# Combining the experts' rows: the second token tile's weighted sum formed on TensorE with diagonal matrices

## The chip, the core and the metric

The kernel runs as one program on one core of a Trainium2 chip. Its time is the device time of one execution in microseconds (us). A core has TensorE (PE in the rows: matrix products into PSUM; PEld is its weight load), VectorE (DVE), ScalarE (ACT), GpSimd (POOL) and SyncE (SP, which here issues the large transfers). Each runs its own instructions in order and waits on semaphores for the others.

## The reference, cut to what matters

Two layers of a diffusion trunk with 256 context and 256 latent tokens, width 1024, all float32. Each layer is an attention mixer and then a mixture of 16 experts, of which each token uses two. What the change touches is the last part of each layer:

```python
w = w / jnp.sum(w, axis=-1, keepdims=True)          # two weights for each token
y = jnp.zeros_like(h)
for e in range(N_EXPERTS):
    a = jax.nn.silu(h @ w_gate[e]) * (h @ w_up[e])
    y = y + gates[:, e:e + 1] * (a @ w_down[e])      # gates is zero but for the two chosen experts
...
x = x + g2 * y.reshape(b, n, d)
...
return rms_norm(x, final_norm_g)
```

So each token's new row is x + g2 * (w1 * y1 + w2 * y2), where y1 and y2 are the outputs of its two experts. Layer 0 does it for context and latent tokens, layer 1 for latent tokens only.

## The kernel before, in words

**Tiles and stages.** Tokens go in tiles of 128: four in layer 0 (two context, two latent), two in layer 1. A layer runs: modulated norm and its transposes (L1546), the QKV products (L1643, each float32 product as three of split parts), attention, the output projection (L1794), the router, the expert blocks (L1878), and then the combination.

**Expert blocks.** A loop over the experts takes blocks of 32 (token, choice) pairs. GpSimd gathers the rows of a block, TensorE multiplies, and GpSimd scatters the results (L766) to the DRAM tensor `expert_rows`. ScalarE copies the last block's result out of PSUM at L1060; TensorE's last work of the loop is two tiny products at L1951, and its last two waits there are for `m_ac` and `m_y`, the second of which is that copy.

**The combination.** When the last scatter has landed, SP issues four transfers of 512 KB (L690): y1 and y2 of tile 0, then y1 and y2 of tile 1, into `val[:, 0..3]`. For each of these two tiles ScalarE multiplies y1 by its per-token weight (`weigh_first`, L860), and VectorE then does three instructions over 128x1024 (`add_experts`): y2 * w2 + y1 (L1162), times the gate row (L1163), plus the kept residual (L1164). The residual of tiles 0 and 1 is kept meanwhile in PSUM banks 1, 2, 6 and 7; that of tiles 2 and 3 of layer 0 is kept in SBUF, in the tensor `moe`, and copied back by ScalarE at L1078. Tile 0 is finished before tile 1, on VectorE's own order. In layer 0 the rows of tiles 2 and 3 are loaded into the same places once tiles 0 and 1 are done (the semaphore `s_cb`), and those tiles are combined later, beside the next layer's products.

**What follows.** In layer 0 ScalarE and VectorE normalise the two context tiles (L837, L854, L1121, L1152, L1153), TensorE turns them (L1546) and starts the QKV products of layer 1. The weights of the first such group are split into two parts before the combination (ScalarE L470, VectorE L473). In layer 1 ScalarE squares the rows (L1092), takes a root (L1094), VectorE scales (L1540), and SP stores.

**Products that nobody reads.** `keep_busy(count)` (L1846) issues `count` products of 128x256 into PSUM bank 3. Their results are not read. The kernel before calls it three times in each layer, around the router.

One float32 product shows as two instructions in the trace: 64 output projection products of layer 0 stand as 128 records of L1794. TensorE's four products of the change, 128x512 each, are so eight records.

Of the kernel before, what the change touches and what calls it, by code (L numbers as in the profile page):

```python
# [31 lines left out]
ALU = mybir.AluOpType  # L32
ACT = mybir.ActivationFunctionType
X_AXIS = mybir.AxisListType.X

P = 128
# [4 lines left out]
LAYERS = 2  # L41
# [33 lines left out]
TILES_OF = [list(range(TILES)), list(range(CTX_TILES, TILES))]  # L75
# [53 lines left out]
def build_trunk(nc, x, c, ctx, c_ctx, ada_w, ada_b, norm1_g, norm2_g, final_norm_g, diff_w_qkv, diff_w_o,  # L129
# [3 lines left out]
    with ExitStack() as stack:  # L133
# [3 lines left out]
        def sem(name):  # L137
            return stack.enter_context(nc.semaphore(name))
# [21 lines left out]
        val = over("val", SET_KB[1] + 32, [P, TILES, D])  # L160
# [16 lines left out]
        resid = sb("resid", [P, TILES, D])  # L177
# [15 lines left out]
        wts = sb("wts", [P, 2, TILES])  # L193
# [4 lines left out]
        ps = stack.enter_context(nc.psum_tensor("ps", [P, 8, 512], F32))  # L198
# [23 lines left out]
        def row(l, piece, t):  # L222

            s = int(t >= CTX_TILES)
            return rows[:, 2 * (piece % 3) + s if l == 0 else LATENT_ROWS[piece]]
# [27 lines left out]
        blk_actT = moe_part(3328, FG).rearrange("p (k s) -> p k s", s=SLOTS)  # L253
        blk_out = [moe_part(3456 + b * DG, DG) for b in range(2)]

        def kept(l, m):

            if m < 2:
                return ps[:, (1, 6)[m]:(3, 8)[m]].rearrange("p a b -> p (a b)")
            return moe_part((m - 2) * D, D)  # L260
# [14 lines left out]
        ident = const("ident")  # L275
# [45 lines left out]
        s_oe = [sem(f"attended_copied_{l}") for l in range(LAYERS)]  # L321
        s_on = sem("heads_normalised")
        s_hs = sem("head_squares")
        s_w1 = [sem(f"first_experts_weighed_{l}") for l in range(LAYERS)]
        s_ot = [sem(f"o_turned_{l}") for l in range(LAYERS)]
        s_oc = [sem(f"o_turned_copied_{l}") for l in range(LAYERS)]
        s_rc = sem("sums_inverted")
        s_wm = [sem(f"wo_products_{l}") for l in range(LAYERS)]
        s_we = [sem(f"wo_added_{l}") for l in range(LAYERS)]
# [13 lines left out]

        s_extra = sem("extra_parts_loaded")
        s_keep = sem("residual_rows_kept")
        m_gu = [sem(f"block_gates_ups_{l}") for l in range(LAYERS)]
        m_dn = [sem(f"block_downs_{l}") for l in range(LAYERS)]
        m_xt = [sem(f"block_in_turned_{l}") for l in range(LAYERS)]
# [7 lines left out]
        s_yl = [[sem(f"expert_rows_loaded_{l}_{b}") for b in range(2)] for l in range(LAYERS)]  # L356
# [99 lines left out]
        def split_weights(eng, l, p, half):  # L456

            g = qkv_jobs[l][[pos[0] for pos in qkv_pos[l]].index(p)][0]
            st = at[l]["qkv", g]
            number = HALF_STRIPS * l + 2 * p + half  # L460
            high = w_high[(2 * p + half) % 3][:]
            ks = slice(half * KC // 2, (half + 1) * KC // 2)
            if eng is nc.scalar:
                wait_strip(eng, l, st)
                if half == 1 and p > 0:
                    eng.wait_ge(s_half, 6 * l + p)
                elif p > 1:
                    first = [pos[0] for pos in qkv_pos[l]].index(p - 1)
                    eng.wait_ge(s_qm[l], first)
                eng.copy(high, strip(l, st)[:, ks]).then_inc(s_whi, 1)  # L470
            else:
                eng.wait_ge(s_whi, number + 1)
                eng.tensor_tensor(w_low[:, strips[l][st][4], ks], strip(l, st)[:, ks], high,  # L473
                                  ALU.subtract).then_inc(s_wlo, 1)
# [73 lines left out]
        NT = [len(t) for t in TILES_OF]  # L548
        HALF = D // 2
# [284 lines left out]
        def _(act):  # L834
# [21 lines left out]
            def weigh_first(l, m):  # L856

                act.wait_ge(s_yl[l][m % 2], 32 * (m // 2 + 1))
                y1 = val[:, 2 * (m % 2)]
                act.activation(y1, y1, ACT.Copy, scale=wts[:, 0, m:m + 1]).then_inc(s_w1[l], 1)  # L860

            for a in range(ADA_QKV // 2):
                copy_mod(a)
# [6 lines left out]
            for l in range(LAYERS):  # L870
# [29 lines left out]
                for n, (g, t) in enumerate(qkv_jobs[l]):  # L900
# [7 lines left out]
                    if qkv_copy[l][n][0] == "act":  # L908
                        m = qk_index[l][n]
# [152 lines left out]
                gate = ps[:, 0, 0:FG]  # L1062
# [12 lines left out]


                for m in range(2, NT[l]):
                    act.copy(resid[:, TILES_OF[l][m]], kept(l, m))  # L1078
                if l == 0:
                    for half in range(2):  # L1080
                        split_weights(act, 1, 0, half)
                for m in range(2):
                    weigh_first(l, m)
                if l == 0:
                    for t in range(CTX_TILES):
                        act.wait_ge(s_cb[0], t + 1)
# [11 lines left out]
        def _(dve):  # L1098
            steps = [0]

            def step(ins):

                steps[0] += 1
                ins.then_inc(s_v, 1)
                dve.wait_ge(s_v, steps[0])
# [49 lines left out]
            def add_experts(l, m):  # L1155

                t = TILES_OF[l][m]
                if l == 0:
                    dve.wait_ge(s_rows, 16 * 8)
                dve.wait_ge(s_w1[l], m + 1)  # L1160
                y1, y2 = val[:, 2 * (m % 2)], val[:, 2 * (m % 2) + 1]
                step(stt(y1, y2, wts[:, 1, m:m + 1], y1, ALU.mult, ALU.add))  # L1162
                step(tt(y1, y1, row(l, 3, t), ALU.mult))  # L1163
                sync(tt(resid[:, t], kept(l, m) if m < 2 else resid[:, t], y1, ALU.add), s_cb[l])  # L1164

            def router_weights(l):
# [9 lines left out]
            for l in range(LAYERS):  # L1176
# [29 lines left out]
                for n, (g, t) in enumerate(qkv_jobs[l]):  # L1206
# [15 lines left out]
                    m = qk_index[l][n]  # L1222
# [301 lines left out]
                if l == 0:  # L1524
                    for half in range(2):
                        split_weights(dve, 1, 0, half)
                for m in range(2):
                    add_experts(l, m)
                if l == 0:
# [14 lines left out]
        def _(pe):  # L1544
# [43 lines left out]
            for l in range(LAYERS):  # L1588
# [363 lines left out]
                        .then_inc(count[l], 1)  # L1952
                pe.wait_ge(m_ac[l], 2 * pairs + 1)
                pe.wait_ge(m_y[l], 2 * pairs + 1)


_INS = ["x", "c", "ctx", "c_ctx", "ada_w", "ada_b", "norm1_g", "norm2_g", "final_norm_g", "diff_w_qkv", "diff_w_o",
# [18 lines left out]
```

## Time and profile before

| | us |
|---|---|
| median of three runs | 1184.06 |
| lowest, highest | 1183.81, 1190.32 |
| the profiled execution's own time | 1184.05 |
| its span in the trace | 1181.9 |

The 2.15 us between the profiled time and its span lie around the traced instructions. Busy time in the span: PE 982.5 us (83%), PEld 658.2, DVE 403.8 (34%), ACT 375.3 (32%), POOL 218.4 (18%). These shares are means over stages with different limits. The change is in two short stages, from about 667 to 688 us and from 1153 to 1178 us, in which TensorE has no work at all, so they are to be read by the chain of waits and in order of time.

### The profile page before, as it was taken

Reading aid. Unit: us, or ns where it says so; the run is one execution under the profiler, and the core shown is the slowest. Engines: PE = TensorE matmul, PEld = TensorE weight load, DVE = VectorE, ACT = ScalarE, POOL = GpSimd, SP = SyncE. Lnnn points to the kernel's source line nnn. Section 1 sums busy time; section 2 is a strip of 40 time slices with the busy share of each in tenths; the row PEclk is TensorE's granted clock in tenths of the full one; section 3 lists DMA queues with packets and bytes.
Section 4 is the critical chain, followed back from the end, with each engine's and each line's share of the span. In section 5 each row is a group of like instructions: output and inputs, shape, how many; then the busy total and the mean of one; then the engine's idle time right before and its main releaser. Section 6 shows DMA issues by size and latency. Waiting matters only on the chain.

```text
span 1181.9 us, 24437 instructions
## 1 busy us (share of the span) xinstructions
PE 982.5 (83%) x9596; PEld 658.2 (56%) x9597; DVE 403.8 (34%) x809; ACT 375.3 (32%) x803; POOL 218.4 (18%) x329
## 2 busy tenths in 40 slices
PE   3699999987789989899899569999999779876650
PEld 1477777544555666466576357787555646553320
DVE  1533330357733532122122373222854512121103
ACT  3532222466621222122222354234842112221102
POOL 0000000000000034244344201910000224442211
PEclk9899999999989999899899869999999889997875
DMA  9766665998230669999999467224447698999972
GB/s 339 254 221 228 226 218 177 335 368 322 88 136 21 220 236 368 422 421 422 425 422 395 171 223 169 72 72 159 198 127 319 262 413 341 411 423 426 424 316 112
DMA packets 93682, 322.07 MB, mean 272 GB/s; under 512 B 21241, under 2 KB 33954, under 8 KB 81330
## 3 DMA queue, kind: packets, MB, share of 16 engines
q1 hardware_dynamic: 85746, 305.40, 67.1%
q0 software_dynamic: 7008, 12.62, 2.9%
q10 hardware_dynamic: 864, 3.15, 0.7%
q8 instruction: 47, 0.77, 0.3%
q14 instruction: 17, 0.14, 0.0%
HBM read 313.67 MB, written 13.99 MB: 277 GB/s over the span
## 4 chain that ended last, share of the span: by engine, by line
PE 66%; DMA 16%; DVE 7%; issue 4%; ACT 3%; SPq 2%; POOL 1%; POOLq 0%; DVEq 0%; ACTq 0%
PE ps L1878 23%; PE ps L1643 21%; DMA expert_sets<-in_moe_w_up_dram 8%; PE ps L1794 7%; PE ps L1546 5%; PE ps L1570 3%; DMA expert_sets<-in_moe_w_down_dram 2%; DMA ring<-in_diff_w_qkv_dram 2%; PE ps L1696 2%; DMA ada_late<-in_ada_w_dram 2%; PE ps L1723 1%; PE ps L1752 1%; DMA expert_rows<-moe,scatter_idx 1%; SPq L590 1%; PE ps L1849 1%
## 5 line engine op out<-in xcount | busy, mean ns | idle before, releaser
L1878 PE MATMUL ps<-expert_sets,moe 128*32 128x256 f32 x6304 | 369.8, 396 | 77.3 <-DMA expert_sets<-in_moe_w_up_dram 47.1
L1878 PEld LDWEIGHTS ps<-expert_sets,moe 128*32 128x32 f32 x6304 | 241.2, 114 | 205.3 <-issue 100.4
L1504 DVE STREAM_TRANSPOSE moe<-moe 128x256 f32<-128x256 f32 x70 | 45.8, 655 | 324.8 <-PE ps L1878 303.1
L1643 PE MATMUL ps<-w_high,x_high 128*128 128x512 f32 x352 | 142.2, 404 | 7.6 <-DVE hT L506 2.7
L1643 PE MATMUL ps<-w_low,x_high 128*128 128x512 f32 x352 | 138.9, 395 | 0.0
L1643 PE MATMUL ps<-w_high,x_low 128*128 128x512 f32 x352 | 138.9, 395 | 0.0
L1068 ACT ACTIVATE moe<-ps 128x128 f32<-128x128 f32 x68 | 18.9, 278 | 270.8 <-PE ps L1878 268.7
L473 DVE TENSOR_TENSOR w_low<-ring,w_high 128x2048 fp32r<-128x2048 f32 x24 | 58.0, 2423 | 131.5 <-ACT w_high L470 131.5
L743 POOL MEMSET moe<- 128x128 f32 x2 | 0.4, 206 | 548.0 <-PE ps L1820 548.0
L766 POOL DMA_INDIRECT expert_rows<-moe,scatter_idx x74 | 75.9, 1026 | 78.3 <-issue 35.5
L1643 PEld LDWEIGHTS ps<-w_high,x_high 128*128 128x128 f32 x352 | 67.1, 191 | 31.9 <-issue 17.4
L761 POOL DMA_INDIRECT moe<-h_rows,gather_idx x68 | 71.2, 1048 | 53.8 <-POOL gather_idx L796 48.9
L1643 PEld LDWEIGHTS ps<-w_high,x_low 128*128 128x128 f32 x352 | 67.1, 191 | 14.5
L1643 PEld LDWEIGHTS ps<-w_low,x_high 128*128 128x128 f32 x352 | 67.1, 190 | 13.1
L1794 PE MATMUL ps<-ring,hT 128*128 128x512 f32 x128 | 58.4, 602 | 0.0
L1060 ACT COPY moe<-ps 128x256 f32<-128x256 f32 x70 | 26.1, 373 | 93.8 <-PE ps L1878 82.8
L470 ACT CAST w_high<-ring 128x2048 fp32r<-128x2048 f32 x24 | 45.7, 1909 | 23.9 <-PE ps L1643 21.1
L1064 ACT ACT_TABLE_LOAD x34 | 43.6, 1283 | 18.8 <-DVE plan L1498 18.2
L936 ACT ACTIVATE hT<-ps,att 128x256 f32<-128x256 f32 (+1 forms) x64 | 36.6, 577 | 27.8 <-DVE att L1250 27.8
L1521 DVE STREAM_TRANSPOSE moe<-moe 128x128 f32<-128x128 f32 x68 | 28.7, 422 | 48.8 <-PE ps L1878 48.6
L1696 PE MATMUL ps<-val,hT 128*128 128x128 f32 x192 | 30.2, 295 | 16.9 <-ACT ao L954 16.9
L1696 PEld LDWEIGHTS ps<-val,hT 128*128 128x128 f32 x192 | 24.6, 196 | 34.5 <-issue 29.6
(235 smaller groups left out, 1103.2 us busy)
## 6 DMA issues: line engine op xcount, KB each, us to landing
expert_sets<-in_moe_w_down_dram SPq DMA_DIRECT2D x32, 2048.0 KB
expert_sets<-in_moe_w_gate_dram SPq DMA_DIRECT2D x30, 2048.0 KB
expert_sets<-in_moe_w_up_dram SPq DMA_DIRECT2D x30, 2048.0 KB
ring<-in_ada_w_dram SPq DMA_DIRECT2D x16, 2048.0 KB, 8.0
ring<-in_diff_w_qkv_dram SPq DMA_DIRECT2D x6, 2048.0 KB, 8.6
ada_late<-in_ada_w_dram SPq DMA_DIRECT2D x6, 2048.0 KB, 13.0
ring<-in_na_w_qkv_dram SPq DMA_DIRECT2D x6, 2048.0 KB, 9.0
rows<-mod_rows SPq DMA_DIRECT2D x12, 512.0 KB, 8.6
```

The costliest lines, as they stand in the source:

```text
L470: eng.copy(high, strip(l, st)[:, ks]).then_inc(s_whi, 1)
L473: eng.tensor_tensor(w_low[:, strips[l][st][4], ks], strip(l, st)[:, ks], high, ALU.subtract).then_inc(s_wlo, 1)
L761: pool.indirect_dma_start(blk_in[b], None, h_rows, bass.IndirectOffsetOnAxis(ap=idx, axis=0), bounds_check=last_row, oob_is_err=False).the ...
L766: pool.indirect_dma_start(made, bass.IndirectOffsetOnAxis(ap=scatter_idx[:, b:b + 1], axis=0), src, None, bounds_check=last_made, oob_is_e ...
L936: act.activation(hT[:, 2 * (u % 3) + cc, 0:nk], ps[:, 2 * (u % 2) + cc, 0:nk], ACT.Exp, bias=att[:, u % 3, cc:cc + 1], accum_out=att[:, u ...
L1064: act.activation(att[:, 0, 3:4], att[:, 0, 0:1], ACT.Silu)
L1504: dve.transpose(blk_inT, blk_in[b].rearrange("p (j k) -> p k j", k=KC)).then_inc(m_xt[l], 1)
L1546: return pe.transpose(dst, src, ident[0:rows_n, 0:rows_n])
L1643: mm = pe.matmul(ps[:, n % 2], x_part[:, k, tok], w_part, start=(k == 0 and i == 0), stop=(k == KC - 1 and i == 2))
L1696: mm = pe.matmul(ps[:, 5, 0:2 * HD], hT[:, 6 + u % 2, k * P:(k + 1) * P], val[:, k, h * 2 * HD:(h + 1) * 2 * HD], start=(k == 0), stop=(k ...
L1794: mm = pe.matmul(ps[:, j % 2], heads_T, strip(l, at[l]["wo", hf])[:, k, :], start=(k == 0), stop=(k == KC - 1))
L1878: mm = pe.matmul(ps[g * SLOTS:(g + 1) * SLOTS, bank, 0:n_out], lhs_T[:, k, :], weights(k, g), start=(k == 0), stop=(k == n_chunks - 1), sk ...
```

## The change

For the second tile (m = 1) of each layer, the sum w1 * y1 + w2 * y2 moves from ScalarE and VectorE to TensorE. VectorE builds two 128x128 diagonal matrices from the identity and the two weights (`weight_diag`). TensorE multiplies them with y1 and y2 in two halves of 512 columns and adds up in PSUM banks 4 and 5 (`weighed`). VectorE then multiplies that by the gate row, straight from PSUM, and adds the kept residual. Ahead of these products TensorE issues 12 unread products (`keep_busy(12)`). The diagonals lie in the first 256 columns of `moe`, where layer 0 keeps the residual of tile 2, so VectorE waits there for ScalarE's copies back (`s_back`). Three semaphores that existed once per layer now exist once.

```diff
+        weight_diag = moe_part(0, 2 * P).rearrange("p (k n) -> p k n", n=P)
+        ON_PE = 1
+        weighed = ps[:, 4:6]
...
-                act.activation(y1, y1, ACT.Copy, scale=wts[:, 0, m:m + 1]).then_inc(s_w1[l], 1)
+                act.activation(y1, y1, ACT.Copy, scale=wts[:, 0, m:m + 1]).then_inc(s_w1[0], 1)
...
                 for m in range(2, NT[l]):
-                    act.copy(resid[:, TILES_OF[l][m]], kept(l, m))
+                    act.copy(resid[:, TILES_OF[l][m]], kept(l, m)).then_inc(s_back, 1)
...
-                for m in range(2):
-                    weigh_first(l, m)
+                weigh_first(l, 0)
...
-                dve.wait_ge(s_w1[l], m + 1)
                 y1, y2 = val[:, 2 * (m % 2)], val[:, 2 * (m % 2) + 1]
-                step(stt(y1, y2, wts[:, 1, m:m + 1], y1, ALU.mult, ALU.add))
-                step(tt(y1, y1, row(l, 3, t), ALU.mult))
+                if m == ON_PE:
+                    dve.wait_ge(s_z, l + 1)
+                    halves, gate = (a.rearrange("p (a b) -> p a b", b=HALF) for a in (y1, row(l, 3, t)))
+                    step(tt(halves, weighed, gate, ALU.mult))
+                else:
+                    dve.wait_ge(s_w1[0], 3 * l + max(m, 1))
+                    step(stt(y1, y2, wts[:, 1, m:m + 1], y1, ALU.mult, ALU.add))
+                    step(tt(y1, y1, row(l, 3, t), ALU.mult))
                 sync(tt(resid[:, t], kept(l, m) if m < 2 else resid[:, t], y1, ALU.add), s_cb[l])
...
+                    dve.wait_ge(s_back, NT[0] - 2)
+                for k in range(2):
+                    ts(weight_diag[:, k], ident, wts[:, k, ON_PE:ON_PE + 1], None, ALU.mult).then_inc(s_diag, 1)
...
                 pe.wait_ge(m_ac[l], 2 * pairs + 1)
                 pe.wait_ge(m_y[l], 2 * pairs + 1)
+                keep_busy(12)
+                pe.wait_ge(s_diag, 2 * l + 2)
+                pe.wait_ge(s_yl[l][ON_PE], 32)
+                for hf in range(2):
+                    for k in range(2):
+                        mm = pe.matmul(weighed[:, hf], weight_diag[:, k], val[:, 2 * ON_PE + k, hf * HALF:(hf + 1) * HALF],
+                                       start=(k == 0), stop=(k == 1))
+                mm.then_inc(s_z, 1)
```

TensorE's order at the end of layer 1 in the changed kernel. A row is the line, the operation, out<-in, the shape, and in brackets the semaphores it waits for.

```order
1957 L1965 MATMUL ps<-cst 32x32 x2
1958 L1967 ISA
1959 L1863 MATMUL ps<-cst 128x256 [waits block_out_1,block_act_1]
1960 L1863 MATMUL ps<-cst 128x256 x11
1961 L1974 MATMUL ps<-val,moe 128x512 [waits expert_rows_loaded_1_1,weight_diagonals]
1962 L1974 MATMUL ps<-val,moe 128x512 x3
```

Everything from the third row on is new. The unread products start behind the wait for `m_y` (`block_out_1`); the four products wait for tile 1's rows and for the diagonals.

VectorE's order in layer 0, from the weight split to the end of tile 1, in the changed kernel:

```order
365 L480 TENSOR_TENSOR w_low<-ring,w_high 128x2048 [waits weights_high] x2
366 L1540 TENSOR_SCALAR moe<-cst,wts 128x128 [waits residual_rows_back]
367 L1540 TENSOR_SCALAR moe<-cst,wts 128x128
368 L1173 SCALAR_TENSOR_TENSOR val<-val,wts 128x1024 [waits first_experts_weighed,rows_loaded]
369 L1174 TENSOR_TENSOR val<-val,rows 128x1024 [waits vector_steps]
370 L1175 TENSOR_TENSOR resid<-ps,val 128x1024 [waits vector_steps]
371 L1170 TENSOR_TENSOR val<-ps,rows 128x1024 [waits expert_rows_weighed,rows_loaded,combined_0]
372 L1175 TENSOR_TENSOR resid<-ps,val 128x1024 [waits vector_steps]
```

Two instructions of 128x128 stand ahead of tile 0, and tile 1 has two instructions of 128x1024 where it had three; the first of them waits for TensorE (`expert_rows_weighed`).

## Rows read from the trace of the kernel before

**Rows 1.** The page: span, and the chain that ended last by engine.

```profile
span 1181.9 us, 24437 instructions
...
PE 66%; DMA 16%; DVE 7%; issue 4%; ACT 3%; SPq 2%; POOL 1%; POOLq 0%; DVEq 0%; ACTq 0%
```

**Rows 2.** The chain of waits at layer 1's end: start, duration, what.

```profile
1164.44 1.16 ACT val L860
...
1168.20 1.24 DVE resid L1164
1169.46 1.30 DVE val L1162
...
1172.04 1.24 DVE resid L1164
```

**Rows 3.** The chain of waits, layer 0's end and layer 1's first products.

```profile
679.97 1.24 DVE resid L1164
...
683.80 1.24 DVE resid L1164
688.11 1.96 PE ps L1546 x8
...
694.49 13.52 PE ps L1643 x48
```

**Rows 4.** In order of time, both ends: start, duration, engine, line [idle before <-releaser].

```profile
667.61 0.37 ACT L1060 COPY moe<-ps 128x256 f32<-128x256 f32 x1 [2.35 <-PE ps L1951]
667.88 1.99 ACT L1078 COPY resid<-moe 128x1024 f32<-128x1024 f32 x2
677.39 1.28 DVE L1162 SCALAR_TENSOR_TENSOR val<-val,wts 128x1024 f32<-128x1024 f32 x1 [1.20 <-ACT val L860]
679.09 1.15 ACT L860 ACTIVATE val<-val,wts 128x1024 f32<-128x1024 f32 x1 [1.81 <-DMA val<-expert_rows]
...
1153.95 0.25 DVE L1518 TENSOR_TENSOR moe<-ps,moe 128x128 f32<-128x128 f32 x1
1155.43 0.37 ACT L1060 COPY moe<-ps 128x256 f32<-128x256 f32 x1 [1.58 <-DMA expert_rows<-moe,scatter_idx]
1167.00 1.15 ACT L860 ACTIVATE val<-val,wts 128x1024 f32<-128x1024 f32 x1 [1.42 <-DMA val<-expert_rows]
```

**Rows 5.** Instructions of L1794: duration in ns min/median/max; then one stretch of them.

```profile
L1794 PE MATMUL ps<-ring,hT x128: 592/592/1061, 336.1 to 401.5; 128*128 128x512 f32 x128
...
880.00:884.00 4.00, 4.00 (x10) 1.71 (x9) 1.00 0.90 258
```

**Rows 6.** L1849 alone by stretch: PE busy (x), PEld, granted clock, DMA share, GB/s.

```profile
914.60:917.90 3.30, 3.30 (x9) 2.65 (x8) 0.50 0.95 357
918.00:921.40 3.40, 3.40 (x17) 3.01 (x16) 1.00 0.96 382
```

**Rows 7.** All engines by stretch: PE, PEld, DVE, ACT, POOL busy (x), clock, DMA, GB/s.

```profile
1143.90:1146.60 2.70, 2.68 (x28) 1.52 (x32) 0.00 (x0) 0.00 (x0) 0.00 (x0) 0.50 0.40 169
1146.70:1151.00 4.30, 3.92 (x74) 2.17 (x64) 1.08 (x3) 0.52 (x2) 0.34 (x2) 1.00 0.04 19
1153.30:1156.80 3.50, 0.00 (x0) 0.00 (x0) 1.21 (x3) 0.91 (x3) 2.14 (x4) 1.00 0.10 37
1156.90:1178.00 21.10, 0.00 (x0) 0.00 (x0) 9.54 (x10) 6.08 (x8) 0.99 (x1) 0.50 0.26 101
667.50:672.10 4.60, 0.00 (x0) 0.00 (x0) 0.40 (x1) 4.49 (x5) 0.99 (x1) 1.00 0.13 47
672.20:688.00 15.80, 0.00 (x0) 0.00 (x0) 13.60 (x14) 7.44 (x10) 0.00 (x0) 0.50 0.65 233
694.50:699.40 4.90, 4.90 (x12) 3.84 (x13) 3.78 (x4) 3.11 (x3) 0.00 (x0) 0.50 1.05 395
```

**Rows 8.** The chain of waits: two of the steps named "issue" beside expert loops.

```profile
475.22 3.41 issue
...
1009.79 3.70 issue
```

More of the change, by code:

```diff
@@ L323, in build_trunk @@
         s_hs = sem("head_squares")
-        s_w1 = [sem(f"first_experts_weighed_{l}") for l in range(LAYERS)]
-        s_ot = [sem(f"o_turned_{l}") for l in range(LAYERS)]
-        s_oc = [sem(f"o_turned_copied_{l}") for l in range(LAYERS)]
+        s_w1 = [sem("first_experts_weighed")]
+        s_ot = [sem("o_turned")]
+        s_oc = [sem("o_turned_copied")]
         s_rc = sem("sums_inverted")
@@ L345, in build_trunk @@
         s_keep = sem("residual_rows_kept")
+        s_back = sem("residual_rows_back")
+        s_diag = sem("weight_diagonals")
+        s_z = sem("expert_rows_weighed")
         m_gu = [sem(f"block_gates_ups_{l}") for l in range(LAYERS)]
```

## The prediction

> **What bounds the kernel now.** I read the page first: TensorE holds 66% of the chain that ended last and VectorE 7% [rows 1]. That is a mean over the program and says little about the two places that the change touches, so I read the chain of waits there, then the instructions in order of time, then the granted clock by stretch.
>
> Layer 1's end: ScalarE starts to weigh tile 0 at 1164.44; VectorE's three steps for tile 0 end at 1168.20 + 1.23 = 1169.43, and its three for tile 1 run without a gap from 1169.46 to 1173.26 [rows 2]. The reader should see that nothing is waited for in tile 1: ScalarE's part of it starts at 1167.00 and takes 1.15 [rows 4], so it is ready 1.3 us before VectorE asks. The path is VectorE itself. Layer 0 is the same: tile 0 ends at 681.20, tile 1 at 685.03, and TensorE starts again at 688.11 [rows 3]; ScalarE's part of tile 1 started at 679.09 [rows 4]. TensorE is idle in both stages, and the granted clock falls there from 1.00 (2.4 GHz) to 0.50 (1.2 GHz), at about 672.1, some 4.7 us after its last product, and at about 1156.9, some 3.5 us after it; it stays there to the end of the stage [rows 7].
>
> **What the change removes.** One VectorE instruction of 1.30 us in each layer (L1162 of tile 1) [rows 2], on the path. One ScalarE instruction of 1.15 us in each layer, off it, worth nothing. In layer 0 ScalarE next waits for tile 0's sum at 681.20, and it had finished its weighing at 680.24, so nothing behind it moves.
>
> **What it adds on VectorE.** Two 128x128 instructions for the diagonals. The nearest row is a two-operand one of that size, 0.25 us [rows 4], so at most 0.5 to 0.6 together. In layer 1 they fall into a stretch where VectorE is busy 1.21 of 3.5 us [rows 7] and then idle until ScalarE has weighed tile 0. In layer 0 they stand between the weight split and tile 0, where VectorE was idle for 1.20 us [rows 4]; ScalarE's copies back, for which they wait, are done at 669.87 [rows 4], 6 us before. Cost nothing; without that cover it would be 0.6. VectorE's gate step now reads PSUM: the residual step of tile 1 reads PSUM too and takes 1.24 us like its neighbours [rows 2], so it costs nothing more. SP's order is the same; the loads of tiles 2 and 3 wait for the same sums as before and move with those; they are combined beside the next layer's products, after the transposes that are delayed too.
>
> **What it adds on TensorE.** First 12 unread products of 128x256, 24 records. They start when ScalarE's last copy is done: 667.98 in layer 0, 1155.80 in layer 1 [rows 4]. At 1.00, 17 records touch 3.40 us; one only reaches in, so 0.21 us each; at 0.50, 0.41 each [rows 6]. So 24 take 5.1 us at full clock and 9.8 at half. In layer 0 the clock is high at the start, and they end at about 673.1. In layer 1 they end at 1160.9 if the clock stays high. There it was granted until 1156.9 with nothing running [rows 7]; if it still falls at 1156.9 and comes back after about as long as elsewhere, they end near 1163.
>
> Then the four products, eight records of 128x512. At 1.00 ten records touch 4.00 us [rows 5], so 4.00 / 9 = 0.44; twice the 0.21 of half the columns is 0.43, which I take, and 0.86 at half clock. They can't start before tile 1's rows are there, at 679.06 and 1166.98 (just before ScalarE started on the same data) [rows 4]. This is the step on which the whole change hangs: from the last unread product to that moment TensorE is idle for 5.9 us in layer 0 and for 4 to 6 us in layer 1, and the rows show the clock falling 3.5 and 4.7 us after the last product [rows 7]. So the products start at, or within a fraction of a microsecond of, half clock. How long they stay there is bounded by two rows: after the start at 1143.92 the clock was back at 1146.7, 2.8 us later; after the one at 694.49 it was still 0.50 at 699.40, 4.9 us later [rows 7]. I take the middle, 3.85 us: 3.85 / 0.86 = 4.5 records at half clock and 3.5 x 0.43 = 1.5 us for the rest, 5.35 us. The last record shows 0.59 us where its share is 0.43 [rows 5], so 0.16 until the result is there: 5.5 us. Bounds: never back in time, 8 x 0.86 + 0.2 = 7.1; clock high all along, 8 x 0.43 + 0.16 = 3.6.
>
> The Trainium skill ("TensorE: Matmul & The Clock Gate", the section "Why this matters for your kernels") asks for no idle gaps between bursts of matmuls, lest the throttle come back: a rule against this change, since the 12 products leave such a gap. The falls in the trace agree with it, 3.5 and 4.7 us after the last product. Had the rows not shown them, I would have taken 3.6 us for the products, and the sum below would be a gain.
>
> **The sum.** Layer 1: products end at 1166.98 + 5.5 = 1172.5, 0.05 for the wait; gate 1.24 and residual 1.24 to 1175.0, against 1173.26: +1.7 us. Layer 0: 679.06 + 5.5 = 684.6, +0.05, +2.5 = 687.1 against 685.03: +2.1. Layer 0's delay stands on the path: the norms, the transposes at 688.11 and the QKV products follow it. One thing is given back there: the QKV products began at 694.49 and ran at half clock until about 699.5 [rows 3, 7]. If the clock returns at the same moment and they start 2 us later, 2 us fewer run at half clock, worth 1 us; if it moves with them, nothing. I take 0.5. Later stages, layer 1's expert transfers too, are started by this chain and shift with it.
>
> Sum: 2.1 - 0.5 + 1.7 = +3.3 us, on the profiled 1184.05, which is the median of the three runs to 0.01: **1187.4 us**. That is 0.3% slower. About 1% (11.8 us) is what a measurement of this kernel tells from no change, so the verdict is "no change".
>
> **The rivals.**
> (a) The clock holds, or the products meet it high. Against it: the idle times above. For it: only that the fall came as late as 4.7 us in one of two places. Then tile 1's sum is there at 1166.98 + 3.6 = 1170.6 in layer 1, and VectorE, free at 1169.43, ends at 1170.6 + 2.5 = 1173.1 instead of 1173.26: -0.15 us. In layer 0 679.06 + 3.6 + 2.5 = 685.2: +0.15. Together 1184.0. Even here the removed 1.30 us come to nothing, since the products take the place of it. If the rows landed 1.2 us sooner against VectorE than they did, the full 1.30 in each layer would be gained, 1181.5. Chance 0.10 for 1181.5 to 1184.5.
> (b) The clock stays low through all the products in both layers: 7.1 instead of 5.5, +1.6 twice, 1190.6, or 1191.1 with nothing given back. For it: 4.9 us at 0.50 in the row at 694.50. Against: the shorter one. Chance 0.15 for over 1189.5.
> (c) Slower by more than 1%: the 32 added product instructions and their waits shift TensorE's code, and its jumps in the expert loops of layer 1 and between stages cost more. The chain has steps in which nothing is waited for, single ones of 3.41 and 3.70 us [rows 8], 4% of it in all [rows 1], 47 us. It decides from a growth of these by a quarter: 3.3 + 11.8 = +15, 1199. Nothing in the rows says that they would grow. Chance 0.02.
> (d) The change doesn't do what it says, the two diagonals or the copies back being late: the cover of 1.20 us and of 6 us would have to be gone; then 0.6 us more, inside the range.
>
> **Numbers.** The forecast, 1185.0 to 1189.5, has 0.73. Its low end is a return after 2.8 us in both layers (4.8 + 0.16 for the products, -0.5 each) and the full 1 us given back: 1187.4 - 1.0 - 0.5 = 1185.9, less 0.9 for what one execution tells. Its high end is about 5 us of low clock in both and nothing given back: 0.5 more each and 0.5 more, 1188.9, and 0.6 beyond. Reaching halfway into (a) and into (b), the range for 8 in 10 is 1184.2 to 1190.3. Within 1%: 0.96; slower by over 1%: 0.03 ((c), and a rest); faster by over 1%: 0.01, since the largest gain in sight, 2.6 us, is 0.2%.
>
> **What would show it.** In the trace after: ScalarE with one weighing fewer in each layer; VectorE idle ahead of tile 1's gate step, released by TensorE, for about 3 us in both layers; the four products starting within 0.1 us of where ScalarE's tile 1 began before, relative to tile 0; granted clock 0.50 at that start; the unread products at an end 4 us or more before it; and TensorE's transposes in layer 0 about 2 us later relative to tile 0's sum. The forecast is wrong if VectorE's wait is under 1.3 us in both layers, or if the difference lies outside these two stages.

## The result and the profile after

| | before | after |
|---|---|---|
| median | 1184.96 us (6 runs) | 1194.8 us (6 runs) |
| lowest, highest | 1183.81, 1190.32 | 1192.64, 1201.32 |
| ratio, 95% interval | | 1.0083, 1.006 to 1.0107 |
| profiled execution, its span | 1184.05, 1181.9 | 1198.58, 1196.6 |

The change costs 0.83%, or 9.8 us (7.1 to 12.7). I had forecast +3.3 us, a range of 1185.0 to 1189.5 and, for 8 in 10, one up to 1190.3: the sign was right, the size was wrong, and "within 1%" held. The profiled execution of after lies 3.8 us above its median, so two more traces of it, and one more of before, stand in a table below; readings that rest on one trace say so.

The page after, the same lines as [rows 1]:

```profile
span 1196.6 us, 24566 instructions
...
PE 66%; DMA 19%; DVE 6%; issue 4%; ACT 2%; SPq 2%; POOL 0%; DVEq 0%; POOLq 0%; ACTq 0%
```

VectorE's share fell from 7 to 6%, as the change wants; the DMA share rose from 16 to 19%. That second number is the first hint that something outside the two layer ends has moved.

Layer 0's end after, in order of time (start, duration, engine, line, [idle before <-releaser]); it answers to [rows 3, 4]:

```profile
667.87 5.42 PE L1863 MATMUL ps<-cst 128*128 128x256 f32 x24 [0.56 <-ACT moe L1067]
675.86 0.48 DVE L1540 TENSOR_SCALAR moe<-cst,wts 128x128 f32<-128x128 f32 x2
679.75 1.23 DVE L1175 TENSOR_TENSOR resid<-ps,val 128x1024 f32<-128x1024 f32 x1
680.07 6.72 PE L1974 MATMUL ps<-val,moe 128*128 128x512 f32 x8 [6.78 <-DMA val<-expert_rows]
686.93 1.23 DVE L1170 TENSOR_TENSOR val<-ps,rows 128x1024 f32<-128x1024 f32 x1 [5.95 <-PE ps L1974]
688.19 1.22 DVE L1175 TENSOR_TENSOR resid<-ps,val 128x1024 f32<-128x1024 f32 x1
```

The unread products took 5.4 us and were over 6.78 us before the rows came. VectorE was done with tile 0 at 680.98 and then idle for 5.95 us, waiting for TensorE. The diagonals cost 0.48 us, hidden. Layer 1's end, which answers to [rows 2, 4]:

```profile
1166.41 7.11 PE L1863 MATMUL ps<-cst 128*128 128x256 f32 x24 [3.56 <-ACT moe L1067]
...
1174.34 1.15 ACT L867 ACTIVATE val<-val,wts 128x1024 f32<-128x1024 f32 x1 [8.07 <-DMA val<-expert_rows]
...
1178.89 6.49 PE L1974 MATMUL ps<-val,moe 128*128 128x512 f32 x8 [5.37 <-DMA val<-expert_rows]
...
1185.48 1.22 DVE L1170 TENSOR_TENSOR val<-ps,rows 128x1024 f32<-128x1024 f32 x1 [6.16 <-PE ps L1974]
```

And the granted clock around the products (columns as in [rows 7]):

```profile
668.00:675.90 7.90, 5.29 (x24) 4.32 (x24) 4.45 (x3) 5.22 (x4) 0.99 (x1) 1.00 0.51 186
676.00:686.10 10.10, 6.03 (x7) 2.52 (x8) 4.07 (x5) 3.49 (x4) 0.00 (x0) 0.50 0.46 171
...
1171.00:1177.60 6.60, 2.51 (x12) 1.88 (x10) 2.05 (x2) 1.15 (x1) 0.00 (x0) 1.00 0.79 292
1177.80:1184.40 6.60, 5.51 (x7) 2.44 (x8) 1.49 (x2) 1.15 (x2) 0.00 (x0) 0.50 0.01 2
```

In both layers the clock went to 0.50 before the products began (from 676 and from 1177.7) and stayed there nearly to their end. So far this is the mechanism that was forecast, in its dearer form.

The part that was not forecast lies between. TensorE in order of time where it enters layer 1's expert loop, first before, then after:

```profile
968.66 2.36 PE L1878 MATMUL ps<-expert_sets,moe 128*32 128x256 f32 x24 [2.52 <-issue]
972.10 37.69 PE L1878 MATMUL ps<-expert_sets,moe 128*32 128x256 f32 x655 [1.08 <-issue]
1013.49 16.77 PE L1878 MATMUL ps<-expert_sets,moe 128*32 128x256 f32 x276 [3.70 <-issue]
```

```profile
970.70 1.93 PE L1892 MATMUL ps<-expert_sets,moe 128*32 128x256 f32 x30 [2.21 <-issue]
979.14 38.43 PE L1892 MATMUL ps<-expert_sets,moe 128*32 128x256 f32 x672 [6.51 <-issue]
1019.53 10.78 PE L1892 MATMUL ps<-expert_sets,moe 128*32 128x256 f32 x196 [1.96 <-issue]
```

"issue" means that the engine waited for nothing that the profile shows. The gap at the loop's entry is 6.51 us instead of 1.08, the one a round later 1.96 instead of 3.70. What a gap there costs is seen on SP, whose next weights wait for TensorE's progress. SP's issue of the last down weights ahead of the first long round, before and after:

```profile
978.27 0.33 SPq L626 DMA_DIRECT2D expert_sets<-in_moe_w_down_dram  x1
```

```profile
986.67 0.33 SPq L633 DMA_DIRECT2D expert_sets<-in_moe_w_down_dram  x1
```

It comes 8.4 us later, where the stage began 2.0 us later. The queue then runs dry during the long round, less full than before (columns as in [rows 7]; the last two are DMA share and GB/s; before, then after):

```profile
985.00:1011.00 26.00, 24.79 (x455) 16.83 (x448) 6.32 (x15) 6.43 (x16) 12.39 (x21) 1.00 0.80 320
```

```profile
993.00:1017.00 24.00, 24.00 (x452) 15.03 (x448) 5.97 (x14) 6.47 (x15) 11.25 (x20) 1.00 0.61 241
```

After it the transfers run at over 410 GB/s to the end in both kernels, so what was not issued there is never caught up. By these two rows the queue stood idle for 0.20 of 26 us before and for 0.39 of 24 us after, 5.2 and 9.4 us; I read the grown DMA share of the chain from this.

### The profile page after: what moved, and what is told of

Read it like the earlier page. It is cut to its first block, busy times and chain, and to the rows that moved or that the text cites. A ratio compares the mean times of both kernels' runs of the same rounds, so it can differ in the third digit from the quotient of the medians.

```text
span 1196.6 us, 24566 instructions
## 1 busy us (share of the span) xinstructions
PE 1001.6 (84%) x9660; PEld 663.4 (55%) x9661; DVE 399.9 (33%) x811; ACT 372.7 (31%) x801; POOL 218.0 (18%) x329
## 4 chain that ended last, share of the span: by engine, by line
PE 66%; DMA 19%; DVE 6%; issue 4%; ACT 2%; SPq 2%; POOL 0%; DVEq 0%; POOLq 0%; ACTq 0%
PE ps L1892 22%; PE ps L1657 21%; DMA expert_sets<-in_moe_w_up_dram 12%; PE ps L1808 7%; PE ps L1560 5%; PE ps L1584 3%; DMA ring<-in_diff_w_qkv_dram 2%; PE ps L1710 2%; DMA ada_late<-in_ada_w_dram 1%; PE ps L1737 1%; DMA val<-expert_rows 1%; PE ps L1766 1%; DMA expert_rows<-moe,scatter_idx 1%; PE ps L1974 1%; SPq L597 1%
## 5 line engine op out<-in xcount | busy, mean ns | idle before, releaser
L1892 PE MATMUL ps<-expert_sets,moe 128*32 128x256 f32 x6304 | 364.5, 392 | 92.4 <-DMA expert_sets<-in_moe_w_up_dram 53.4
L1892 PEld LDWEIGHTS ps<-expert_sets,moe 128*32 128x32 f32 x6304 | 233.7, 113 | 222.6 <-issue 112.3
L1863 PE MATMUL ps<-cst 128*128 128x256 f32 x186 | 47.2, 416 | 4.1 <-ACT moe L1067 4.1
```

What stands on the lines that cost most here:

```text
L1863: pe.matmul(ps[:, 3, 0:2 * P], ident, cst[:, 0:2 * P], start=True, stop=True)
L1892: mm = pe.matmul(ps[g * SLOTS:(g + 1) * SLOTS, bank, 0:n_out], lhs_T[:, k, :], weights(k, g), start=(k == 0), stop=(k == n_chunks - 1), sk ...
```

## The table that the experiments are read by

Four numbers of each trace, in us. **End 0** and **end 1** are the ends of the two layers, from ScalarE's first weighing of tile 0 to the end of VectorE's last step of tile 1 (a different start of SP or of the scatter doesn't enter). **Products**: the four products in layer 0 / layer 1. **Stage**: from the first to the last expert product of layer 1, with the gap at the loop's entry / the gap a round later. "Records" counts TensorE instructions (products and weight loads, so four for each float32 product) added ahead of layer 1's loops.

| trace | records | end 0 | end 1 | products | stage | gaps |
|---|---|---|---|---|---|---|
| before | 0 | 8.90 | 8.82 | | 214.2 | 1.1 / 3.7 |
| before again (r_before) | 0 | 8.90 | 8.82 | | 215.6 | 1.9 / 3.5 |
| e1_layer1_only | 0 | 8.90 | 10.99 | - / 5.16 | 214.0 | 2.2 / 3.5 |
| e3_no_unread | 16 | 11.82 | 12.74 | 5.98 / 6.50 | 217.3 | 2.6 / 3.8 |
| e4_unread_only | 48 | 8.90 | 8.83 | | 216.4 | 5.0 / 2.4 |
| after | 64 | 13.50 | 13.62 | 6.72 / 6.49 | 221.8 | 6.5 / 2.0 |
| after again (r_after) | 64 | 11.97 | 11.53 | 6.06 / 5.37 | 219.4 | 6.5 / 2.6 |
| after, third (r2_after) | 64 | 11.54 | 11.21 | 5.30 / 5.78 | 221.7 | 6.6 / 1.8 |
| e2_layer0_only | 64 | 11.85 | 8.82 | 6.04 / - | 216.6 | 6.1 / 1.9 |
| e8_quarter | 64 | 8.90 | 8.83 | | 221.4 | 6.4 / 1.9 |
| e5_bridged | 120 | 9.88 | 10.37 | 3.67 / 3.60 | 218.4 | 5.0 / 1.2 |
| e6_bridged_halves | 120 | 8.88 | 9.01 | 3.60 / 3.67 | 218.4 | 5.9 / 1.3 |
| e9_half | 128 | 8.90 | 8.82 | | 218.4 | 5.5 / 1.3 |
| p192 | 192 | 8.90 | 8.82 | | 215.7 | 2.0 / 3.1 |
| p256 | 256 | 8.90 | 8.82 | | 216.9 | 2.8 / 3.6 |
| e11_halves_whole | 256 | 9.24 | 9.80 | 3.67 / 3.60 | 215.7 | 2.2 / 3.4 |
| e7_whole_fetch | 256 | 10.90 | 10.75 | 5.33 / 5.31 | 215.8 | 2.1 / 3.5 |
| e7 again (r2_whole_fetch) | 256 | 10.86 | 10.64 | 5.47 / 5.12 | 216.1 | 2.3 / 3.9 |

## The experiments

**One layer at a time.** The diff is a condition on the layer around the change.

```diff
+        PE_LAYERS = (1,)          # and (0,)
+        def on_pe(l, m):
+            return m == ON_PE and l in PE_LAYERS
```

> The change in layer 1 alone; layer 0 combines as before, so TensorE's instructions ahead of layer 1's expert loops are those of the kernel before. Theory P (placement): of the +9.8 us (median), 2 come from layer 0's end, 4 to 5 from layer 1's end, and the rest from TensorE waiting for nothing visible at the start of layer 1's expert loops (steps 'issue' of 3.10, 2.47, 2.21 and 6.51 us after, against 2.15, 2.52, 1.08 before), because instructions were added ahead of these loops. Then this one is +4 to +5 us (ratio 1.003 to 1.0045), its tail the longer one and its issue steps those of before. Theory C (chance): the issue steps differ from execution to execution whatever the code, and the two ends carry all of the difference: layer 1's end would then have to be worth more, +6 to +7 us. Theory D: the unread products disturb the loading of the expert rows, whose second tile came 1.2 and 2.0 us later against the first than before; then the second tile's rows are late here too in layer 1.

> The change in layer 0 alone; layer 1 combines as before. Theory P: +2 us at layer 0's end and +3 to +6 us in the steps named issue of layer 1's expert loops, so +5 to +7 us (ratio 1.004 to 1.006). Theory C: +2 us (1.001 to 1.0025), issue steps scattered. Theory D: the second tile's rows in layer 0 about 1.2 us later than before against the first tile's.

Measured: layer 1 alone 1.003 (1.0015 to 1.0045), +3.6 us; layer 0 alone 1.0049 (1.0031 to 1.0067), +5.8 us. Together 9.4 of the 9.8: the two parts add up, within intervals of about 2 us on each. Layer 1 alone has the stage and the gaps of before; layer 0 alone has the 6.1 us gap at the loop's entry, though nothing of it lies in layer 1. Theory P's ranges of time held (layer 1 at the low edge); the 4 to 5 us that it gave layer 1's end did not, which is 2.2 us longer in e1's trace. Theory C fails on layer 0's part.

**The unread products, away and alone.**

```diff
-                keep_busy(12)                       # e3: the change without them
```

```diff
                 pe.wait_ge(m_y[l], 2 * pairs + 1)
+                keep_busy(12)                       # e4: the kernel before, with them and nothing else
```

> The change without its 12 unread products (both layers). The four products then run at half clock, as they do anyway in the profile after (6.7 us in layer 0, 6.5 us in layer 1), unless the clock comes back during them. Theory D: without unread products the second tile's rows land as soon as before (2.6 to 3.0 us after the first tile's), and the kernel gains 2 to 3 us on the changed one. Theory P: fewer instructions ahead of layer 1's loops (8 records instead of 32 per layer); the issue steps are somewhere between before and after. Theory C: within 1 us of the changed kernel, 0.8% over before.

> The kernel before with the 12 unread products at each layer's end and nothing else: nobody waits for them. By what stands on the path it costs nothing: 0 us, or -1 us if the clock is higher at the QKV products that follow. Theory P: +3 to +6 us, all of it in issue steps in layer 1's expert loops, since 24 records stand ahead of them. Theory C: 0. Theory D: the expert rows land 1 to 2 us later, both tiles or the second, at both ends: +1 to +3 us.

Without them 1.0057 (1.0034 to 1.008), against 1.0083 with them: the intervals overlap. **The 12 unread products buy nothing in the kernel's time**; TensorE is idle for 3.7 to 6.8 us behind them and the clock falls. What they do to the products differs by layer: in layer 0 these take 6.0 us without them and 5.3 to 6.7 with them, in layer 1 6.5 us without them (one trace) and 5.1 to 6.5 with them (six traces), so up to 1 us may be bought there. Theory D falls by its reason, though not by the time, which came out some 3 us under the changed kernel's, where D had 2 to 3: the rows of tile 1 came 3.22 and 3.65 us after those of tile 0 without unread products, and 2.77 and 2.60 with them in the kernel before. Alone they give 1.0017 (0.9998 to 1.0036), 0 to 4 us: under the 3 to 6 us that P expected, not to be told from nothing by time, but the trace has the gaps of P (5.0 / 2.4).

**The clock bridged.**

```diff
-                keep_busy(12)
+                keep_busy((26, 24)[l])
...
+                    for hf in range(2):             # e6 only: VectorE's gate step by halves
+                        dve.wait_ge(s_z, 2 * l + hf + 1)
+                        cols = slice(hf * HALF, (hf + 1) * HALF)
+                        step(tt(y1[:, cols], weighed[:, hf], row(l, 3, t)[:, cols], ALU.mult))
...
+                    mm.then_inc(s_z, 1)             # e6 only: after each half
```

> The changed kernel with 26 (layer 0) and 24 (layer 1) unread products instead of 12, so that TensorE is busy until just before the second tile's rows land. Theory K (clock): the four products take 6.0 to 6.7 us in every trace so far because they start at half clock; bridged they start at full clock and take 3.5 to 3.7 us, so each layer's end is 2 to 3 us shorter, and the kernel is 4 to 6 us faster than the changed one: +0.3 to +0.5% over the kernel before, and no gain on it, since the products then just take the place of the removed step and the instructions ahead of layer 1's loops are still there. Rival (the products are slow for another reason, such as their operands or the wait): still over 5 us each and no change.

> As the bridged kernel, and VectorE's gate step works in two halves, the first as soon as TensorE has its 512 columns, so that it runs beside TensorE's second half. Theory K: 0.5 to 1 us a layer better than the bridged kernel: each end 0.3 to 1 us shorter than in the kernel before. In all 0 to +0.2% over the kernel before, because of the about 2 us that the instructions ahead of layer 1's expert loops cost. Rival: as for the bridged kernel.

Bridged 1.0032 (1.0012 to 1.0052), halves 1.0035 (1.0015 to 1.0054). In the trace of the second, by stretch, and its VectorE in layer 0:

```profile
667.50:679.30 11.80, 11.26 (x52) 9.87 (x53) 6.78 (x6) 7.01 (x6) 0.99 (x1) 1.00 0.53 196
679.40:683.00 3.60, 3.54 (x9) 1.27 (x8) 2.44 (x3) 1.77 (x3) 0.00 (x0) 1.00 0.23 59
```

```profile
681.36 0.69 DVE L1171 TENSOR_TENSOR val<-ps,rows 128x512 f32<-128x512 f32 x1 [0.18 <-PE ps L1975]
683.05 0.69 DVE L1171 TENSOR_TENSOR val<-ps,rows 128x512 f32<-128x512 f32 x1 [0.99 <-PE ps L1975]
683.77 1.22 DVE L1176 TENSOR_TENSOR resid<-ps,val 128x1024 f32<-128x1024 f32 x1
```

At 1.00 the products take 3.6 to 3.7 us in all six cases (e5, e6, e11), and in the fourteen where the clock is at 0.50 from the start (in one, from 0.1 us after it) 5.1 to 6.7. So the products' length is shown to be a matter of the clock. Theory K held for e5. For e6 it missed: it gave 0 to +0.2% and ends 0.3 to 1 us shorter than before's, and measured are +0.35%, no less than e5, and ends of 8.88 and 9.01 us against 8.90 and 8.82. That is the ceiling: with clock and halves both, the ends are those of the kernel before. In e5 layer 1 the rows of tile 1 had landed at 1175.82 and the unread products ran to 1177.37, 1.6 us too long; a bridge has a length to miss on both sides.

**Second and third traces.**

> The kernel before once more, for a second trace. If the expert stage of layer 1 (first to last product) is worth 214 us whatever the execution and 216 to 222 with instructions added ahead of it (placement), it is 214 here again. If it scatters by several us from execution to execution (chance), it may be anything from 213 to 218. The QKV stage of layer 1, 124.8 us in the profile before and 121.7 to 122.6 in the five others, tells which of these was the odd one.

> The changed kernel once more, for a second trace. Placement: expert stage 216 to 217 us, not the 221.8 of the first profile (an execution 3.8 us above the median), products 6 to 6.8 us, the second tile's rows later than the first's by 2.7 to 3.3 us and not by 4.2 and 4.6. If these come out as in the first profile, the late rows belong to the change and not to chance.

> The changed kernel again, side by side with the next one: +0.7 to +0.9% over before; stage 218 to 222 us; ends 11 to 13.5 us each where before has 8.9.

Before again: 1183.49 us, stage 215.6. Its rows of tile 1 came 3.58 and 3.28 us after tile 0's (2.96 and 2.56 in the first trace), and its ends are to the hundredth the same, 8.90 and 8.82: ScalarE's slack of 1.3 us swallows them. After again: 1197.05 us, stage 219.4, above what I gave placement. Third: 1.0072 (1.0046 to 1.0098), and the stage 221.7. So the long stage of the first profile was no accident, though r_after shows that it moves by 2 us between executions.

**How much code, or where.** 32x32 unread products, four records each, at layer 0's end, where TensorE is idle.

```diff
+                for _ in range(16 if l == 0 else 0):     # 16, 32, 48, 64 on the kernel before
+                    pe.matmul(ps[0:SLOTS, 3, 0:SLOTS], ident[:, 0:SLOTS], ident[:, 0:SLOTS], start=True, stop=True)
```

> The kernel before with 16 unread products of 32x32 at layer 0's end (64 records, a quarter of a fetch: the insertion of the changed kernel, without its waits, its long products or their clock). Theory P: expert stage 216.5 to 219 us, a gap of 5 to 6.5 us at the loop's entry and 1 to 2.5 us a round later; +2 to +4 us in all. Rivals P2 and C: P2 the same or less, C 214 to 216 as in the two traces of before.

> The kernel before with 32 unread products of 32x32 at layer 0's end (128 records, half a fetch). Theory P: gaps of another pattern than either; the stage anything from 213 to 220. P2: more than with 16 products, by as much again. C: 214 to 216.

> The kernel before with 48 unread products of 32x32 at layer 0's end: 192 records, three quarters of a fetch. Theory P makes no forecast of its size, only that it may differ from both neighbours (213 to 220 us for the stage), and that its time over before is that of its stage within 1.5 us. P2: between 128 and 256 records, so +3 us or more.

> The kernel before with 64 unread products of 32x32 at layer 0's end: 256 records, one whole fetch. Theory P (where the code lies): expert stage 214 to 216 us, the 3.5 us gap one round after the loop's entry, and 0 to +1 us in all. P2 (how much was added): 219 us or more and +4 us or more, as 64 records gave +4.6 us and 128 gave +2.8 us.

Time over before: 64 records 1.0039 (1.0018 to 1.006), 128 records 1.0024 (1.0006 to 1.0041), 192 records 1.0014 (0.9991 to 1.0037), 256 records 1.0017 (1.0002 to 1.0032). **Sixteen tiny products that nobody waits for cost 4.6 us (2.1 to 7.1).** TensorE in that trace:

```profile
965.81 1.93 PE L1878 MATMUL ps<-expert_sets,moe 128*32 128x256 f32 x30 [1.39 <-issue]
974.15 39.23 PE L1878 MATMUL ps<-expert_sets,moe 128*32 128x256 f32 x672 [6.42 <-issue]
1015.25 15.09 PE L1878 MATMUL ps<-expert_sets,moe 128*32 128x256 f32 x272 [1.86 <-issue]
```

and with 256 records:

```profile
976.76 1.50 PE L1878 MATMUL ps<-expert_sets,moe 128*32 128x256 f32 x24 [1.08 <-issue]
981.10 35.82 PE L1878 MATMUL ps<-expert_sets,moe 128*32 128x256 f32 x655 [2.84 <-issue]
1020.49 9.88 PE L1878 MATMUL ps<-expert_sets,moe 128*32 128x256 f32 x148 [3.57 <-issue]
```

Theory P2 (the amount) falls: the stage is longest at 64 records and short again at 192 and 256, and the pair of gaps goes back to that of before. Two sizes missed what was expected: the stage at 64 records (221.4, where P had 216.5 to 219) and the time at 256 (+2.0 us, 0.2 to 3.8, where P had 0 to +1). The trace shows instructions coming in pieces of 16 KB on a queue of their own (q8); that they are TensorE's is inferred from their pace, in straight-line code one for every 180 to 340 of its records. In the changed kernel 8 of them come in the 52 us from 940 us, beside weights at 400 to 450 GB/s:

```profile
q8 instruction: 8, 0.13, 1.0%
```

The kernel before has 8 of them in the same stretch as well, so it isn't their number that grew. The gaps go with their moments. In all 18 traces the gap a round later ends 2.3 to 2.8 us after the start of a piece. The gap at the entry ends 2.3 to 2.6 us after one in nine traces, and 4.5 to 4.6 us after one in the nine others: those with 64 to 128 records, and p192. After, for example, a piece starts at 974.6 and TensorE goes on at 979.1; before, one starts at 969.8 and it goes on at 972.1.

The Trainium skill ("Runtime: NRT & Kernel Launch", the section "Instruction fetch mechanics") says that instructions are refilled in blocks of 16 KiB or 256 instructions, that crossing a block is mostly hidden, and that a taken branch to a block not at hand stalls the engine. The traces agree with the size. They agree that a crossing in straight-line code is hidden: from 60 to 400 us and from 700 to 930 us none of the 18 has a gap named "issue". The gaps of 1 to 6.6 us stand in the loops, where the code branches, and fit the stall; a trace doesn't name the branch, so that it is the cause is argued.

**The two remedies together, and the changed kernel with a whole block.**

```diff
+                for _ in range(34 if l == 0 else 0):     # e11: behind the products of e6
...
-                keep_busy(12)                            # e7: in layer 0, 60 products of 32x32 for 12 of 128x256
```

> The bridged kernel in halves (its two ends were 8.88 and 9.01 us in the trace against 8.90 and 8.82 before), with 34 unread products of 32x32 behind the real ones in layer 0, so that 256 records are inserted, one whole fetch. Theory P: both ends as before and the expert stage at 214 to 216 us: the time of the kernel before, within 1 us. P2 or C: +0.35% as without the 34.

> The changed kernel; in layer 0 its 12 unread products of 128x256 are replaced by 60 unread products of 32x32, so that with the four real products 256 TensorE records are inserted ahead of layer 1's loops instead of 64. In straight-line code the trace has a 16 KB instruction fetch about every 250 records, so this moves the code by about one whole fetch instead of a quarter. Theory P, in its sharper form (what counts is where the expert code lies against the 16 KB pieces): layer 1's expert stage is back at 214 to 216 us, with a gap of 1 to 2.6 us near entry of the loop (about 975) and 3.5 us one round later, and the kernel is 2 to 4 us faster than the changed one. Rival P2 (what counts is how much code was added): 219 us or more. Rival C (chance): anything from 214 to 222 with no pattern in the gaps. The products' clock as before: 6 us and more.

> The changed kernel with 256 instead of 64 records inserted ahead of layer 1's loops, again. Theory P: stage 214 to 216 us, and 2 to 5 us faster than r2_after on the same chip, so +0.4 to +0.6% over before. Chance, or P2: no faster than r2_after.

e11: 1.0007 (0.9989 to 1.0025), the kernel before within what can be told, as P expected, though its ends in the trace are 9.2 and 9.8. It is the bridged kernel in halves (1.0035) and 34 tiny products more, and these bring the stage from 218.4 to 215.7 us. e7: stage and gaps as P expected, twice (215.8 and 216.1), but the time a miss both times: 1.007 (1.0041 to 1.0098) and 1.0066 (1.0041 to 1.0091), where 1.004 to 1.006 was expected and its neighbour r2_after had 1.0072. A part of it is seen in the second trace: from layer 0's last expert product to ScalarE's first weighing it takes 10.3 us, and 10.7 in p256 and 10.0 in p192, where fourteen of the others take 8.6 to 8.8. An instruction piece falls into the rows' transfer there:

```profile
q8 instruction: 1, 0.02, 0.5%
...
val<-expert_rows SPq DMA_DIRECT2D x4, 512.0 KB, 6.3
```

(p256, 671 to 683 us; before has no q8 line in that stretch and 5.1 us to landing). So the padding brings the stage back by 3 to 5 us and can take 1.3 to 2 us ahead of it, which may be most of the 1.7 and 2.0 us that p192 and p256 cost. The first trace of e7 has the piece too, 3.4 us after the last expert product where the other three have it at 3.7 to 3.9, and takes 8.9.

The rest of the miss is open, and single traces can't settle it, because they scatter ahead of the change: up to layer 0's last expert product, where the work is the same in all, the 18 traces take 664.7 to 672.9 us. From there to the end of the span the two of before take 514.5 and 514.6, the three of after 529.4, 524.9 and 523.4, and the two of e7 520.0 and 521.7. By these, padding the changed kernel is worth 2 to 9 us; by the times of all runs, nothing that can be told.

## Why the prediction was wrong

Means of the three traces of after, against the traces of before ([rows 2, 3] and the second one; stage and QKV with e1 as a third):

| | forecast | measured |
|---|---|---|
| layer 0's end | +2.1 | 12.3 - 8.9 = +3.4 |
| layer 1's end | +1.7 | 12.1 - 8.8 = +3.3 |
| given back in QKV | -0.5 | -1.2 (122.2 against 123.4, traces scatter by 3) |
| layer 1's expert stage | 0 | 221.0 - 214.6 = +6.3 |

The step that failed is the last row of this table. The prediction said that layer 1's expert transfers "are started by this chain and shift with it", and so put the stage at nothing; it grew by 6.3 us. The sum of the four is +11.8, and these traces' own times are 11.4 us apart (1195.2 on average against 1183.8); the medians of all runs are 9.8 apart.

**The removed step, the diagonals, the PSUM operand, ScalarE's slack**: right. 0.48 us for two diagonals (0.5 to 0.6 forecast), 1.22 us for the gate step from PSUM (1.24).

**The clock**: right in kind, a little mis-sized. The products meet 0.50 in all traces that don't bridge, and take 5.8 us on average over fourteen (5.1 to 6.7), where 5.5 was forecast with 3.6 and 7.1 as ends. In the three traces of after they take 6.0 us in layer 0 and 5.9 in layer 1, 0.5 and 0.4 more than forecast.

**The products' start**: mis-sized. I took the moment at which ScalarE had started on tile 1 in one trace, 2.96 and 2.56 us after tile 0 [rows 4]. The three traces of after have 4.16, 3.29, 3.62 and 4.55, 3.58, 2.83. Before had such values too (3.58, 3.28 in the second trace) and nothing came of them, because ScalarE had 1.3 us in hand. The change took a transfer with slack and put it on the path, and I priced it by one trace. That is the other 0.8 us of layer 0's end and 1.1 of layer 1's. The spread explains only a part: over the sixteen ends that combine as before the interval is 2.5 to 3.6 us and 2.9 on average, so its mean would have added 0.2 us, and the six of after average 3.7. Whether the rows are later because of the change is open. VectorE's wait for TensorE was 5.95 and 6.16 us in the first trace, where about 3 was forecast.

**Rival (c)** is the mechanism that the forecast left out. I named it (added products shift TensorE's code and its jumps in layer 1's loops cost more) but let it decide only from a growth by a quarter of all such steps, gave it a chance of 0.02, and costed it at nothing below that. The prediction's own sign of being wrong, a difference that lies outside the two stages, came true for about half. It is neither all nor nothing: 64 records at layer 0's end, alone, are worth +4.6 us (2.1 to 7.1), about half of the result. The forecast treated the added instructions as hidden because TensorE was idle when they ran; they were hidden there, and paid for almost 300 us later, where pieces of instructions come beside weights at over 400 GB/s. The sum of the issue steps doesn't tell the kernels apart either (in the first 90 us of the stage 9.4 and 11.4 us in the traces of before, 16.2, 11.7 and 15.6 in those of after); what does is which one grows: the one at the loop's entry, behind which SP's next weights wait. That the longer stage comes from this wait is read from traces; no run moved the gap alone.

**Rival (a)**, that the products meet the clock high, is shown false for this kernel and true for the bridged one, where it isn't worth the 1184.0 that (a) gave (e5 is +0.32%); **(b)** comes near in the first profile (6.7 and 6.5 of the 7.1) and not in the third (5.3 and 5.8). **The verdict within 1%** held, with 9.8 of 11.8 us used up.

## What to carry to other kernels

Instructions that an idle engine executes are not free if they shift the code of a later loop: compare the gaps named "issue" at the loops' entries in both traces, and test a suspected shift with a few tiny products that nobody reads. Work moved to TensorE after a pause is to be priced at half clock (here after 3.7 us of idle time and more), and a burst to keep the clock up helped only where it lasted until the work started, or to 1.1 us before. When a transfer loses its slack, price it by several traces, and expect it to be later still: here even its spread was not enough.

## What was not expected of the hardware

- TensorE's gap at the loop's entry was 1.1 to 2.8 us with 0, 16, 192 or 256 records inserted and 5.0 to 6.6 us with 48 to 128, in 18 traces without an exception; the gap a round later goes the other way, 3.1 to 3.9 against 1.2 to 2.6.
- The stage was 214.0 to 216.9 us with 0, 192 or 256 records, 217.3 with 16, and 216.4 to 221.8 with 48 to 128.
- In the three traces where a 16 KB piece of instructions starts 3.7 to 3.9 us after layer 0's last expert product, just as the four transfers of 512 KB are issued, ScalarE's first weighing comes 10.0 to 10.7 us after that product; in the one where the piece starts at 3.4 us it comes at 8.9, and in the fourteen without a piece there at 8.6 to 8.8. That the piece is the cause is likely by this, and not shown.
- From 60 to 400 us and from 700 to 930 us, in straight-line code, no gap of TensorE is named "issue" in any of the 18 traces, though a piece comes for every 180 to 340 records.
